# Moving each values unit of the latent attention behind the next query block's turn and scores

## What is computed

```python
proj = h @ w_in                                   # shared input projection
# mixer 1: latent attention, 8 heads; keys and values come from a 256-wide latent
s = (q_lat . ckv + q_rope . krope) * SM_SCALE     # prompt: causal by chunks of 64
p = softmax(s);  o_attn = (p @ ckv) @ w_uv
# mixer 2: RWKV-7, a state recurrence over the tokens, 8 heads of 64
S = S * w_t + sa (kk_t a_t)^T + v_t k_t^T;  y_t = S r_t
out = concat(o_attn, o_rw) @ w_out                # then norm, gate, residual, SwiGLU
```

## Time and profile before

| What | Value |
|---|---|
| median of 3 runs | 2451.12 us (2450.7 to 2462.66) |
| the profiled execution | 2452.57 us, of which the recorded span is 2450.6 us |
| TensorE busy over the span | 2016.9 us, 82% |
| VectorE, ScalarE, GpSimd busy | 940.8, 646.9 and 203.5 us |
| mean granted TensorE clock | 0.911 of full speed |
| the mixed stage's prompt jobs, four pairs | 556.8 to 652.0, 760.7 to 841.6, 958.0 to 1038.9 and 1148.7 to 1238.2 us |

### The profile page before, as it was taken

One profiled execution on the slowest core, in us unless ns is written; L12 is line 12 of the kernel. 1 busy time (PEld: TensorE's weight loads), 2 busy tenths in 40 slices (PEclk: granted clock), 3 DMA queues, 4 the chain that ended last, 5 costly groups with the idle time before them and its releaser, 6 DMA issues. The chain is left out here.

```text
span 2450.6 us, 39448 instructions
## 1 busy us (share of the span) xinstructions
PE 2016.9 (82%) x16286; PEld 1764.8 (72%) x16286; DVE 940.8 (38%) x1433; ACT 646.9 (26%) x1251; POOL 203.5 (8%) x287
## 2 busy tenths in 40 slices
PE   4799974198888889879865397599999999999985
PEld 3799942166667657657643395499999999999984
DVE  2222245445344425434523615423332333323336
ACT  5323341123323323323323313521111101111101
POOL 0000000032223112312300000100000000000000
PEclk8899996599899989989987699799999999999998
DMA  6111035601000001000019211111111101111022
GB/s 246 43 43 43 26 79 152 172 26 42 17 29 30 17 17 43 17 16 19 4 53 353 95 44 57 58 45 34 52 52 51 34 18 52 52 51 35 24 92 73
DMA packets 112109, 147.46 MB, mean 60 GB/s; under 512 B 65921, under 2 KB 80897, under 8 KB 111521
## 3 DMA queue, kind: packets, MB, share of 16 engines
q1 hardware_dynamic: 111968, 145.41, 18.3%
HBM read 114.90 MB, written 30.50 MB: 59 GB/s over the span
## 5 line engine op out<-in xcount | busy, mean ns | idle before, releaser
L1859 PE MATMUL ps<-hhi,whi 128*128 128x364 f32 (+1 forms) x1056 | 348.6, 330 | 30.9 <-DVE hlo L1098 27.9
L1859 PE MATMUL ps<-hlo,whi 128*128 128x364 f32 (+1 forms) x1056 | 348.4, 330 | 0.0
L1859 PE MATMUL ps<-hhi,wlo 128*128 128x364 f32 (+1 forms) x1056 | 348.4, 330 | 0.0
L347 DVE TENSOR_TENSOR wlo<-wraw,whi 128x1024 fp32r<-128x1024 f32 x72 | 88.0, 1225 | 521.8 <-ACT whi L343 521.8
L360 PE MATMUL ps<-hhi,whi 128*128 128x364 f32 (+1 forms) x672 | 222.8, 332 | 68.5 <-DVE wlo L347 36.7
L1859 PEld LDWEIGHTS ps<-hhi,whi 128*128 128x128 f32 x1056 | 199.7, 189 | 31.8 <-DVE hlo L1098 28.5
L360 PE MATMUL ps<-hlo,whi 128*128 128x364 f32 (+1 forms) x672 | 222.6, 331 | 0.0
L360 PE MATMUL ps<-hhi,wlo 128*128 128x364 f32 (+1 forms) x672 | 222.3, 331 | 0.0
L1836 PE MATMUL ps<-ahi,dhi 128*128 128x364 f32 x528 | 180.1, 341 | 25.4 <-DVE acc L1438 16.8
L1859 PEld LDWEIGHTS ps<-hlo,whi 128*128 128x128 f32 x1056 | 199.8, 189 | 0.0
L1859 PEld LDWEIGHTS ps<-hhi,wlo 128*128 128x128 f32 x1056 | 199.5, 189 | 0.0
(11 more groups left out here) (206 smaller groups left out, 3045.8 us busy)
## 6 DMA issues: line engine op xcount, KB each, us to landing
wraw<-in_w_tiles SPq DMA_DIRECT2D x72, 512.0 KB, 3.4
late<-in_ada_w SPq DMA_DIRECT2D x8, 2048.0 KB, 9.7
ci<-scan SPq DMA_DIRECT2D x17, 768.0 KB, 4.5
draw<-in_w_down SPq DMA_DIRECT2D x22, 512.0 KB, 3.4
slab<-in_ada_w SPq DMA_DIRECT2D x4, 2048.0 KB, 18.5
scan<-mix SPq DMA_DIRECT2D x12, 512.0 KB, 4.3
x<-in_x_t SPq DMA_DIRECT2D x4, 1456.0 KB, 9.7
x<-x_mid SPq DMA_DIRECT2D x1, 4352.0 KB, 14.2
```

The source lines that it names most:

```text
L347: nc.vector.tensor_tensor(wlo[u][:, :, :], wraw[u][:, :, :], whi[u][:, :, :].bitcast(F32), ALU.subtract).then_inc(w_lo, 1)
L1859: mm = nc.tensor.matmul(ps[:, 3 * u + c, 0:n], w[u][:, k, :], x[:, k, a:a + n], start=(k == 0 and w is whi and x is hhi), stop=(k == KD - ...
```

## The change

In `job_units`, the values unit of job jb - 1 now comes behind the turn of job jb and the scores of job jb + 2, for jb from 1 to 15. Behind turn 15 come V14 and V15 both. The sample's jobs 16 and 17 keep their order. Nothing else is changed: the same units with the same costs, on all three engines. The order becomes S0, S1, T0, S2, T1, S3, V0, T2, S4, V1, T3 and so on, up to T14, V13, T15, V14, V15, S16. Since `interleave` counts costs in the order of this list, the recurrence steps fall at other places among the units as well.

```diff
@@ -83,7 +83,10 @@
             units.append(("scores", jb + 2, 0))
         if jb == PJOBS:
             units.append(("scores", jb + 1, 0))
-        units.append(("values", jb, 0))
+        if 1 <= jb < PJOBS:
+            units.append(("values", jb - 1, 0))
+        if jb >= PJOBS - 1:
+            units.append(("values", jb, 0))
     return units
```

## The result

The changed kernel takes 2461.89 us (median of 20 runs, 2454.4 to 2468.99) against 2455.78 us for the kernel before (20 runs, 2447.86 to 2463.87). The ratio is 1.0027, with a 95% interval of 1.0016 to 1.0038: slower by 6.6 us by the ratio and by 6.1 us by the two medians, less than half a per cent. A second set of runs of the changed kernel gave 1.0019 (1.0008 to 1.0029). The ratios compare fast executions only; a few far slower ones of the kernels further down are left out. The median of three runs with which the prediction worked, 2451.12, was near the low end of what the kernel before does.

A forecast was written before the change was run, and what follows sets the result against it. TensorE, busy 82% of the span, was taken as the bound, so only its waits and clock count. Waits +1.3 and clock +3 gave +4.3 on 2452.57, thus 2456.9; less 1.45 for the median, about 2455, range 2443 to 2466.

The forecast's parts named there:

- The target: Values units in all four pairs: their waits for ScalarE's copy, 7.9 us together, would all go.
- V1's 0.89: Start of a pair: V1's wait of 0.89 us would only move, becoming 0.75 at T2.
- the four stretches: Prompt jobs of pairs 0 to 3 in the mixed stage: idle time should read about 8, 12, 12 and 10.5 us.
- The four new waits of pairs 1 and 2: Steps t1 to t4 would wait for the copy to `xt` behind the exponentials of the scores, 3.74 us per pair.
- -3.7 predicted: Pair 0: TensorE's waits would fall from 10.2 to 6.5 us, as steps and turns meet different neighbours.
- "+2.7 us each": Pairs 1 and 2: waits would rise from 7.5 to 10.2 us each, through steps t and adjacent turns.
- "a values unit uses a copy that is a whole job old": Values units after the change: with so old a copy, all 7.9 us of their waits go.
- The clock: Pair 3: a fall to 1.2 GHz behind the new wait may cost nothing or 5 us; 3 was taken.
- 3.0 predicted: Pair 3: x0 behind S15 and `turns` would wait 3.0 us for three copies queued behind the exponentials.
- Rival 2: Clock falls to 1.2 GHz once in each of pairs 1 and 2, 5 in pair 3: +16, 2467 us; chance 0.13.
- waits of +1.3: All four pairs: changes in TensorE's waits of -3.7, +5.4 and -0.4 us sum to +1.3, plus or minus 4.5.
- Rival 1: Only the values waits go and the moved steps cost nothing: 2451.1 - 7.9 = 2443 us; chance 0.08.

The follow-up runs named there:

- experiment 2: Kernel before with its old order of units, but the recurrence steps where the changed kernel has them; ratio to the kernel before 1.0018.
- experiment 1: Changed kernel with the new values order, but each recurrence step kept behind the same place as before the change; ratio to the kernel before 0.998.
- experiment 5: Changed kernel with steps x1 to x5 due behind a job's scores put ahead of them, in jobs 7 to 15; ratio to the kernel before 0.9989.
- experiment 7: Changed kernel's unit order, steps of jobs 8 to 15 placed one behind each turn group, none directly behind scores from job 10; ratio to before 0.9988.

## Why the prediction was right

**The target.** All 7.9 us of values waits for ScalarE went, as predicted, and V1's 0.89 came back as 0.67 at T2 (0.75 predicted).

**The steps.** The forecast for the idle time of the four stretches was 8, 12, 12 and 10.5 us; measured 7.6, 13.1, 13.1 and 10.9. The four new waits of pairs 1 and 2 were to be 0.77, 1.08, 0.86 and 1.03 and are 0.77, 1.01, 0.80 and 1.03. In experiment 2, where a longer values unit covers the second and the fourth, these are 0.80 and 0.82: the tile that the cover lost is the difference of 0.21. That they exist through the moved steps, and not through the values units, experiments 1 and 2 show. That they are the queue behind the exponentials, ScalarE's rows and experiment 5 show. Pair 0: -3.7 predicted; in idle time 11.6 - 7.6 = -4.0.

**The term that was too small** is "+2.7 us each" for pairs 1 and 2, which measured 3.7 in idle time. The larger part is V2 and V4, which wait for the copy-out of bank 5 (0.9 us in all). The step that failed is "a values unit uses a copy that is a whole job old": this looked only at the wait for `pt`, and not at the second wait of the same unit, for `put_out`, whose distance on TensorE had become one job shorter. Another 0.2 is at T10.1 (0.87 instead of 0.68), where by the order of ScalarE's list the copies of the solve come first; this cause is read from the list, and no run tests it.

**The clock.** Taken as +3 for pair 3, between 0 and 5. The fall came, behind a wait of 3.08 us (3.0 predicted), but it lasted 3.6 us and not 11: at a mean of 0.54 it cost about 1.7 us (3.60 x 0.46), and with the wait removed the busy time fell by 1.4 to 1.9. So the term was too large, and made up for the one that was too small. Rival 2, a fall in pairs 1 and 2, did not come: they read 1.00 in both profiles of the changed kernel, with four waits of up to 1 us and the turns' between. (Pair 0's clock of 1.0, on which the prediction leans here, holds from 575 us on; over the whole stretch have 0.95.) By the rule of the Trainium skill ("Perfetto Trace Analysis", "Matmul Optimizations"), that power follows the matmul engine's utilization, more waits could have cost clock there as well. In these two pairs the trace shows no fall; in the kernel of experiment 1, with less idle time, it shows a little (0.98 and 0.96). So here the amount of idle time does not order the stretches by clock.

**The total.** +4.3 us predicted, 4.7 in the stretches, 4.7 to 6.6 in the two ratios. That the sum came out so close is in part luck: waits of +1.3 and a clock term of +3 were predicted, and the stretches have +3.3 of idle time and +1.4 of busy time. The time of 2455 is the other way about: it started from a median of three, 2451.12, that lay 4.7 us below the median of 20, and so stands 6.9 us under the measured 2461.89. Rival 1 (only the values waits go) gave 2443; experiment 1, which holds the steps in place, takes 2450.66 and is the nearest thing to it. Its idle time fell by 4.3 us and not by 7.9, since waits came back at T2, in pair 0 and in pair 3.

## What to carry to other kernels

Where an order is computed from costs, moving one unit also moves everything that is interleaved with it, and that can outweigh the move: write out both orders and look at the neighbours. An operation that another engine waits for should stand ahead of the long one in its queue (the copy of 0.36 us behind exponentials of 1 us), but each swap takes cover from something else, and the queue of the next engine sets how far this goes. Here the move with the steps held in place (0.998) and with x ahead too (0.9975) is faster than both kernels by the intervals, by a quarter of a per cent or less against the kernel before.

## What the runs showed of the hardware that I had not expected

The granted clock falls in stretches that are no more idle than others that keep it. Pair 2 reads 0.96 with 7.4 us idle of 81 in experiment 1, and 1.00 with 13.1 us idle of 85 in the changed kernel, and pair 1 reads 0.96 with 9.5 us idle of 84.5 in experiment 7 where pair 2, in the same loop body, reads 1.00:

```profile
758.00:842.50 84.50, 74.96 (x891) 0.96 0.08 26
959.00:1041.20 82.20, 72.09 (x890) 1.00 0.08 25
```

The two execute the same instructions, and the lengths differ by 2.3 us. The fall lies in the first 20 us of pair 1 (0.73 and then 0.93 by tens of us, 1.00 from there on), where T0 has waited 1.9 us for VectorE. In experiment 1 it lies at the same place in pair 2 (0.75 and 0.90). But pairs 1 and 2 of the kernel before have the same wait of 1.9 us at a clock of 1.00, so that wait alone does not decide it, and what does stays open. A difference of this size in one pair is no evidence for an edit unless the clock is the same on both sides.
